# A three-layer fp32 model on one core: another signal for Down's operand, a moved weight load, four gather buffers

## The reference

```
def swiglu(h, w_gate, w_up, w_down):
    return (jax.nn.silu(h @ w_gate) * (h @ w_up)) @ w_down
...
    for e in range(N_EXPERTS):
        he = jax.nn.silu(xt @ w_gate[e]) * (xt @ w_up[e])
        y = y + combine[:, e:e + 1] * (he @ w_down[e])
...
        x = x + y.reshape(B, T, D)
    return _rmsnorm(x, final_norm)
```

## Time and profile before

| | us |
|---|---|
| three timed runs | 2007.46, 2011.48, 2014.10 |
| their median | 2011.48 |
| the profiled execution | 2009.65 |
| its span, first to last instruction | 2007.7 |
| what lies around the span | 1.95 |

### The profile page before, as it was taken

The page is one execution under the profiler, slowest core; times in us unless marked ns, Lnnn a source line. Parts: engine busy times, 40 slices in busy tenths (PEclk is TensorE's granted clock), DMA queues, the critical chain, the costliest instruction groups (busy, mean ns, idle before and its releaser), DMA issues. The chain is left out here.

```text
span 2007.7 us, 22052 instructions
## 1 busy us (share of the span) xinstructions
PE 1851.7 (92%) x9136; PEld 1394.8 (69%) x9136; DVE 762.5 (38%) x1110; ACT 581.9 (29%) x888; POOL 171.0 (9%) x216
## 2 busy tenths in 40 slices
PE   6998999999999957899899999999999996999992
PEld 5777888878778847677788887877777784333330
DVE  4325222233454342553622223354236553332233
ACT  4325222222442141353522223243235520000001
POOL 4000000000000010010000000000000201333322
PEclk9979999999999975699999999999999996999996
DMA  7203333322133311801233332224231027999973
GB/s 212 85 31 85 85 104 98 90 87 102 63 105 105 89 44 40 267 1 43 63 105 85 103 104 84 103 75 130 80 118 43 8 103 276 378 378 396 387 312 138
DMA packets 182369, 261.24 MB, mean 130 GB/s; under 512 B 19112, under 2 KB 139080, under 8 KB 169744
## 3 DMA queue, kind: packets, MB, share of 16 engines
q1 hardware_dynamic: 158928, 204.66, 30.7%
q0 software_dynamic: 19328, 26.06, 4.2%
q10 hardware_dynamic: 4032, 29.36, 3.8%
HBM read 297.82 MB, written 29.40 MB: 163 GB/s over the span
## 5 line engine op out<-in xcount | busy, mean ns | idle before, releaser
L147 DVE TENSOR_TENSOR RING_R<-RING,RING_R 128x2048 fp32r<-128x2048 f32 (+1 forms) x110 | 249.9, 2275 | 686.6 <-ACT RING_R L144 686.6
L166 PE MATMUL PB<-RING_R,OPS_R 128*128 128x512 f32 (+1 forms) x1056 | 413.9, 392 | 11.2 <-DVE OPS_R L469 5.1
L167 PE MATMUL PB<-RING_R,OPS_R 128*128 128x512 f32 (+1 forms) x1056 | 410.2, 388 | 0.0
L168 PE MATMUL PB<-RING_R,OPS_R 128*128 128x512 f32 (+1 forms) x1056 | 410.1, 388 | 0.0
L144 ACT ACTIVATE RING_R<-RING 128x2048 fp32r<-128x2048 f32 (+1 forms) x110 | 208.5, 1898 | 406.0 <-DMA RING<-in_ffn_w_down 141.7
L166 PE MATMUL PB<-OPS_R,RING_R 128*128 128x512 f32 (+1 forms) x736 | 282.3, 384 | 7.8 <-DVE OPS_R L270 7.8
L167 PE MATMUL PB<-OPS_R,RING_R 128*128 128x512 f32 (+1 forms) x736 | 281.7, 383 | 0.0
L168 PE MATMUL PB<-OPS_R,RING_R 128*128 128x512 f32 (+1 forms) x736 | 281.5, 383 | 0.0
L166 PEld LDWEIGHTS PB<-RING_R,OPS_R 128*128 128x128 f32 x1056 | 200.0, 189 | 54.4 <-issue 7.8
L168 PEld LDWEIGHTS PB<-RING_R,OPS_R 128*128 128x128 f32 x1056 | 199.6, 189 | 40.9
L167 PEld LDWEIGHTS PB<-RING_R,OPS_R 128*128 128x128 f32 x1056 | 200.1, 189 | 39.6
(11 more groups left out here) (347 smaller groups left out, 1970.3 us busy)
## 6 DMA issues: line engine op xcount, KB each, us to landing
RING<-in_ffn_w_gate SPq DMA_DIRECT2D x44, 512.0 KB, 4.0
RING<-in_ffn_w_up SPq DMA_DIRECT2D x44, 512.0 KB, 5.3
RING<-in_ffn_w_down SPq DMA_DIRECT2D x44, 512.0 KB, 3.9
RING<-in_w_expert_gate SPq DMA_DIRECT2D x16, 1024.0 KB
RING<-in_w_expert_up SPq DMA_DIRECT2D x16, 1024.0 KB
OPS<-in_w_expert_gate SPq DMA_DIRECT2D x16, 1024.0 KB
OPS<-in_w_expert_up SPq DMA_DIRECT2D x16, 1024.0 KB
Y<-in_w_expert_down ACTq DMA_DIRECT2D x14, 1024.0 KB
```

The lines of the kernel that those rows point to most:

```text
L147: nc.vector.tensor_tensor(RING_R[:, raw], RING[:, raw], RING_R[:, high].bitcast(fp32), ALU.subtract).then_inc(s_wlo, 1)
L166: nc.tensor.matmul(o, x[0], w[0], start=start, stop=False)
L167: nc.tensor.matmul(o, x[0], w[1], start=False, stop=False)
L168: return nc.tensor.matmul(o, x[1], w[0], start=False, stop=stop)
```

## The change

There are three edits.

**The operand of Down.** A new signal `rows01` is given by the matmul of the last hidden tile that reads rows 0 and 1 of the operand for the last time (up, kk = 1). ACT's `split_hidden(0)` waits for it, and no longer for the end of the up product. DVE's low part of the same pair moves ahead of the product of the last hidden tile. PE, in Down's first row, waits for that product before row tile 2, which writes the banks 4 and 5 that the product reads.

**The head.** On SP the two DMAs of weight chunk 0 move ahead of tile 1 of x.

**The end.** R1 and R2 hold four tiles, so the eight gathers are issued without a wait. DVE sums tile 0, and then sums tile m and norms tile m - 1 in turn. ACT runs one more root ahead of the first squares, on two words of `stat`.

```diff
@@ Down.pe
                         for m in range(MT):
+                            if self.ffn and (j, kk, m) == (0, 0, 2):
+                                pe.wait_ge(*self.ffn.hid.at(FT + 3))
                             t = tile(j, kk, m)
@@ Down.split_hidden, Down.splits
                 if name == "act":
                     eng.wait_ge(*f.hid.at(3 + 2 * j + 2))
-                    eng.wait_ge(*(f.um.at(FT) if j < 4 else self.free.at(j - 3)))
+                    eng.wait_ge(*(f.rows01.at(1) if j == 0 else f.um.at(FT) if j < 4 else self.free.at(j - 3)))
...
-                if self.ffn:
+                if self.ffn and name == "act":
                     self.split_hidden(eng, name, 0)
@@ GateUp.pe
+                            if last and (t, kk) == (1, 1):
+                                x.then_inc(self.rows01.sem, 1)
@@ GateUp.dve
                     split_chunk(dve, "dve", self.n0 + k + 2, it)
+                    if isinstance(it, int) and it * 3 + k == FT - 1:
+                        down.split_hidden(dve, "dve", 0)
                     dve.wait_ge(*self.sl.at(it * 3 + (k + 1)))
                     dve.wait_ge(*self.um.at(it * 3 + (k + 1)))
@@ last_pool
             for m in range(MT):
-                if m >= 2:
-                    pool.wait_ge(*l_a.at(2 * (m - 1)))
                 for k, r in enumerate((R1, R2)):
                     nc.gpsimd.indirect_dma_start(
-                        r[:, m % 2, :], None, slot_dram[:, :],
-                        bass.IndirectOffsetOnAxis(ap=si[:, k, m:m + 1], axis=0)).then_inc(l_g[m % 2], 16)
+                        r[:, m, :], None, slot_dram[:, :],
+                        bass.IndirectOffsetOnAxis(ap=si[:, k, m:m + 1], axis=0)).then_inc(l_g[m], 16)
@@ last_dve
+            summed(0)
+            for m in range(1, MT):
+                summed(m)
+                normed(m - 1)
+            normed(MT - 1)
@@ last_act
         def last_act(act):
+            nc.scalar.activation(stat[:, 62:63], stat[:, 60:61], ACT.Sqrt)
@@ block.sync
             sp.dma_start(X[:, 0, :], x_v[:, 0, :]).then_inc(s_x[0], 16)
+            load_chunk(sp, 0)
             sp.dma_start(X[:, 1, :], x_v[:, 1, :]).then_inc(s_x[1], 16)
-            load_chunk(sp, 0)
```

More of the change, by code:

```diff
@@ L583, in __init__ @@
                 self.um = Sig("ffn_up_mm", FT)
+                self.rows01 = Sig("ffn_rows01_read", 1)
                 self.sl = Sig("ffn_silu", FT)
@@ L622, in tile @@
                 def tile(it, k):
-                    n = self.n0 + k
+                    n, last = self.n0 + k, isinstance(it, int) and it * 3 + k == FT - 1
                     wait_split(pe, n, it)
@@ L646, in act, with dve @@
                 split_done["act"] = self.n0 + FT + 2
-            def dve(self, dve):
+            def dve(self, dve, down):
                 split_to(dve, "dve", self.n0 + 2)
@@ L2184, in moe_dve @@
                 rows_out(s)
-        l_g = [sem("token_rows0"), sem("token_rows1")]
+        l_g = [sem(f"token_rows{m}") for m in range(MT)]
         l_a = Sig("down_x", 2 * MT)
@@ L2193, in program @@
         s_out = sem("out_stored")
-        R1 = RING[:, 0:2 * D].rearrange("p (s n) -> p s n", s=2)
-        R2 = RING[:, 2 * D:4 * D].rearrange("p (s n) -> p s n", s=2)
+        R1, R2 = [RING[:, i * MT * D:(i + 1) * MT * D].rearrange("p (m n) -> p m n", m=MT) for i in range(2)]
         def last_pool(pool):
@@ L2201, in last_pool, with summed, normed @@
             for m in range(MT):
-                if m >= 2:
-                    pool.wait_ge(*l_a.at(2 * (m - 1)))
                 for k, r in enumerate((R1, R2)):
                     nc.gpsimd.indirect_dma_start(
-                        r[:, m % 2, :], None, slot_dram[:, :],
-                        bass.IndirectOffsetOnAxis(ap=si[:, k, m:m + 1], axis=0)).then_inc(l_g[m % 2], 16)
+                        r[:, m, :], None, slot_dram[:, :],
+                        bass.IndirectOffsetOnAxis(ap=si[:, k, m:m + 1], axis=0)).then_inc(l_g[m], 16)
         def last_dve(dve):
             wait_gain(dve, 5)
-            for m in range(MT):
-                dve.wait_ge(l_g[m % 2], 32 * (m // 2 + 1))
-                nc.vector.scalar_tensor_tensor(X[:, m, :], R1[:, m % 2, :], w1_[:, m, :], X[:, m, :], ALU.mult, ALU.add
+            def summed(m):
+                dve.wait_ge(l_g[m], 16 * 2)
+                nc.vector.scalar_tensor_tensor(X[:, m, :], R1[:, m, :], w1_[:, m, :], X[:, m, :], ALU.mult, ALU.add
                                                ).then_inc(l_a.sem, 1)
                 dve.wait_ge(*l_a.at(2 * m + 1))
-                nc.vector.scalar_tensor_tensor(X[:, m, :], R2[:, m % 2, :], w2_[:, m, :], X[:, m, :], ALU.mult, ALU.add
+                nc.vector.scalar_tensor_tensor(X[:, m, :], R2[:, m, :], w2_[:, m, :], X[:, m, :], ALU.mult, ALU.add
                                                ).then_inc(l_a.sem, 1)
-            for m in range(MT):
+            def normed(m):
                 dve.wait_ge(*l_st.at(m + 1))
@@ L2404, in _ @@
             d_ev.dve(dve, n2)
-            f0.dve(dve)
+            f0.dve(dve, d_f0)
             d_f0.dve(dve, n3)
@@ L2415, in _ @@
             d_od.dve(dve, n4)
-            f1.dve(dve)
+            f1.dve(dve, d_f1)
             d_f1.dve(dve, n5)
```

## The result

The changed kernel's median is 1998.28 us (six runs, 1992.63 to 2005.22), against 2011.20 for the kernel before (six runs, 2007.46 to 2014.10). The ratio is 0.9934, with an interval of 0.9911 to 0.9956, so 13 us faster, between 9 and 18. I had forecast 8.4 us and 1999 to 2008. The profiled execution took 1993.87 us with a span of 1991.9.

The account below looks back on a forecast made before the run. PE was taken as the bound, busy 1851.7 of 2007.7 us, so only its idle times and the two ends count. Terms -3.7 - 1.7 + 1.0 - 4.0 = -8.4 from 2011.48 gave 2003.1, range 1999 to 2008.

Parts of the forecast that it names:

- Part 1, the stop: Start of Down in both feed-forwards: PE's stop shrinks from 2.56 to 0.72 us, 3.7 us less in all.
- The clock behind the stop: After Down's first stop: the granted clock no longer falls to 0.50, 1.7 us less, bounds 0 and 3.4.
- Part 2, the head: Program start: chunk 0's split still waits for x's tile 1, landing at 12.8, so 1.0 us lost.
- Part 3, the end: Final gathers, sums and norms: the last norm ends at 2000.55 and not 2004.61, 4.0 us less.
- The bound on the landings: Last gathers: if the DMA is the limit, each tile's pair lands 3.0 us after the last, at 1989.9 and 1992.9.
- The sum: Whole kernel: -3.7 - 1.7 + 1.0 - 4.0 = -8.4 us, so 2003.1, rounded 2003.
- A step won or lost early therefore moves everything behind it: Whole kernel: no stage between the ends starts at a fixed time, so the three edits' effects add up.
- (e): Moved dense stretches keep the clock at 0.50 for over 17 us; 25 us would give 2015.6, slower; chance 0.05.
- (a): The clock falls after all, at Down's start or elsewhere; everything but the 1.7 holds: -6.7, 2004.8; chance 0.22.
- (b): End or head pays less: tile 1 at 13.24, tile 3 late by 1 us, one clock fall: 2006.3; chance 0.12.
- (c): Head gains: ACT has tile 1 when the chunk lands at 10.4, split 1.4 early: -10.8, 2000.7; chance 0.06.
- (d): At the end DVE holds off POOL's gathers 7 and 8; end 2.6 later than before: 2009.7; chance 0.03.

Follow-up runs that it names:

- the two kernels that take these falls away near PE's old start: Kernel before plus 13 transposes filling PE's stop: 1.0002. Kernel with Down's operand alone changed plus 21 transposes ahead of Down: 0.9988.
- a late PE: Kernel with Down's operand alone changed, plus transposes delaying PE: 21 ahead of Down, 0.9988; 38 in the first feed-forward only, 0.9985.
- the buffers alone: Kernel before with four gather buffers and root's table ahead, all sums ahead of all norms: 29.3 us from last row store's issue to the end.

## Why the prediction was right and wrong

**Part 1, the stop.** Right. PE stops for 0.61 us (0.72 forecast), which is 1.95 us less and not 1.84, in each feed-forward. The product of the last hidden tile is late next and costs nothing, as said: PE never stops at the new wait.

**The clock behind the stop.** Right at the place, wrong as a term of the total. The falls behind the stops are gone: 10 behind 14 stops of the old operand, none behind 13 of the new one, 2.4 us on average where I had 1.7. But the two kernels that take these falls away near PE's old start gained +0.4 (between -2.0 and +2.6) and -1.4 beside PE's own 1.0, and spent no less time at the lower level. What the clock gives comes with the moved start and over the whole kernel, not behind the stops alone.

**Part 2, the head.** Right. The edit does what it says, and it costs time. The first half of chunk 0 took tile 1's old place, at 6.7, and tile 1 took the last, at 13.2, nearly the 13.24 of equal bytes. I had put it at 12.8. The split came 1.3 us late (1.0 forecast, bounds 0.3 and 1.5), and 1.5 late over three profiles, two of them beyond the bound. The rule of the Trainium skill on turns between queues (DMA: Bandwidth & Descriptors, Queues, rings and completion order) had spoken for 12.05; the measurement decides, and by it tile 1's larger rows gained nothing: 186 packets carried the bytes that 296 had carried.

**Part 3, the end.** Right in size, wrong in one cause. DVE's part is 16.9 us and not 20.7, with 16.7 forecast. Over many profiles the end gives 4.7 us where I said 4.0. But I gave the norms between the sums a part in it, and no trace shows one beside four buffers. The bound on the landings (3.0 us from one tile to the next) was too slow; with the buffers alone DVE sums without a gap behind tile 1.

**The sum.** The traces show 3.9 us for the stops, 4.7 for the end and -1.5 for the head, 7.1 together. With the 2.4 of the falls behind the stops it would be 9.5, against 8.4 forecast, and that alone would have given 2002, inside the range. Measured are 12.9 and 12.5. The failing step is "A step won or lost early therefore moves everything behind it", with nothing else happening to what is moved, and with it a clock term of 1.7 us set at one place, the stop. What the runs show in its place: the stages behind get shorter as well. The attention of the second block takes 76.6 us in both profiles of the changed kernel, and 79.7 and 78.1 in the two of the kernel before (80.3 over the nine profiles with the old operand or a late PE), so 2 to 4 us less. Over twelve timed runs of the changed kernel, span x (1 - clock) is 106.1 us on average, against 111.8 over 91 runs of the kernel before, so 5.7 less, twice the standard error about 3. 2.4 of that is the shorter end, which leaves 3.3 for the clock elsewhere, twice the forecast. 7.1 and 3.3 make 10.4. The last 2 us or so are within the intervals (9 to 18 for the first comparison) and stay open.

**The rivals.** (e), the clock moved by the shift, came nearest, with the wrong sign: I had priced it as a loss over one long dense stretch and not as a gain in a stage of short stops. It belonged in the range on both sides, and the lower end should have been near 1995, 3 to 4 us below my 1999. (a) and (b), both smaller gains, didn't come. (c) wanted tile 1 of x when the chunk lands, at 10.4; it came at 13.2. (d), POOL held off by DVE, was real in kind and harmless in size. I had read the rows wrong: of the gathers at 1986.78 and 1988.02 the first began ahead of DVE's sum and the second 0.11 us before its end, so neither tested it. Gathers 7 and 8 of the changed kernel begin under a running sum and take 1.12 and 1.02 us, until 0.81 after that sum's end. POOL is held for one DVE instruction and not for the whole chain of them, so (d)'s 2.6 us of loss did not come.

## What to carry to other kernels

Before you move a load ahead, read what stands before its first reader: the chunk came 2 us earlier here and its reader waited for what had been moved behind it. When a queue is slow, look for small loads beside it before you change its order; that gave 3 us where the order cost 1.5. Where you argue that one engine does not hold another, check that the second one started while the first was running. A clock fall seen in one profile is one draw: count it over several executions, don't take its removal for a gain of the total, and let the range take in what a shift of a few microseconds does to the stages behind, in both directions.

## What was unexpected

- The length of the second block's attention has few values, equal to 0.1 us from one execution to another, and which of them comes goes in part with the time of entry. What picks the value is left open. The even mixer, at 104 us, has such values too: 19.9 us in 13 of 16 profiles, 17.1 in two and 18.0 in one. The changed kernel had 17.1 in its first profile and 19.9 in its second, so it is no steady part of the gain.
- A gain in the router is largely given back. In five of the six profiles with the new operand and no added delay the router took 4.1 us less than in the kernel before (7.7 and not 11.8), and the stretch behind it 2.5 to 3.6 more, because PE then waits longer for the gathered rows: in the changed kernel 7.6 us and not 5.3. Five of the ten other profiles have the short router too, so the operand does not make it.

```profile
PE PB L2093 <- DMA Z<-h_rows,idx_i: 7.6, 1, 7.6
```

- A gather issued while DVE sums or norms waits for that one DVE instruction. Of the 128 last gathers in the sixteen profiles, 26 begin with 0.19 to 1.09 us of a sum or norm still to run. Each ends 0.81 to 0.82 us after that instruction's end, and so takes 1.01 to 1.90 us. The 102 others take 0.94 to 0.98; two of them begin within 0.03 us of the sum's start and are not held. In the kernel with sums and norms in turn and two buffers the first gather of tile 2 ends at 1988.94, 0.81 after the sum's 1988.13, and the first of tile 3 at 1992.05, 0.81 after the norm's 1991.24:

```profile
1986.85 1.28 DVE L2213 SCALAR_TENSOR_TENSOR X<-RING,Z,X 128x1024 f32<-128x1024 f32 x1
...
1987.20 1.74 POOL L2205 DMA_INDIRECT RING<-expert_rows,slot_i  x1 [5.28 <-DVE X L2216]
...
1989.95 1.29 DVE L2223 SCALAR_TENSOR_TENSOR Y<-X,stat,GP 128x1024 f32<-128x1024 f32 x1
...
1990.56 1.49 POOL L2205 DMA_INDIRECT RING<-expert_rows,slot_i  x1 [0.30 <-issue]
```

  The Trainium skill (SBUF — State Buffer, SBUF: two separate sides) says that a DVE instruction with two inputs in SBUF and a GpSimd instruction that reads SBUF lock each other out, for the whole instruction of whichever starts first. The traces agree for a DVE instruction that is already running.
